# Layer-0 FFN norm by token halves with its differences between the scalings, and a state-space output block moved to a scratch slot

## The reference, cut to what matters

```python
# first block: state-space mixer, then its output projection under a gate
y_ssm = _mamba2_mixer(hn @ w_z, hn @ w_xbc, hn @ w_dt, ...) @ w_ssm_out      # 2048 -> 1024
merged = jax.nn.sigmoid(hn @ w_gs) * y_ssm + jax.nn.sigmoid(hn @ w_ga) * y_nsa

# second block, layer i
x = x + g1 * ox                      # ox: grouped-query attention times gqa_w_out in layer 0
x = x + g2 * conv_ffn(norm_modulate(x, norm2_g[i], sh2, sc2), ffn_w_up[i], ...)
def norm_modulate(h, g, shift, scale): return rms_norm(h, g) * (1 + scale) + shift
def conv_ffn(h, w_up, conv_w, conv_b, w_down):
    u = dwconv_centred(h @ w_up, conv_w, conv_b)          # three taps along the tokens
    val, gate = jnp.split(u, 2, axis=-1)
    return (jax.nn.silu(gate) * val) @ w_down
```

## Time and profile before

| | |
|---|---|
| median of 3 runs | 2077.77 us (2075.35 to 2079.31) |
| profiled execution | 2078.08 us, span 2076.2 us |
| mean granted TensorE clock | 0.979 |
| TensorE busy | 1947.4 us, 94% of the span |
| VectorE, ScalarE, GpSimd busy | 1027.1, 561.2, 59.5 us |
| read from HBM | 354.97 MB, 171 GB/s over the span |
| chain that ended last | PE 88%, DVE 4%, DMA 3%, issue 2% |

### The profile page before, as it was taken

How to read it: one execution, slowest core, us unless ns; L and a number is a source line. 1 busy time by engine, 2 the same in 40 slices (tenths; PEclk the granted TensorE clock), 3 DMA queues, 4 the chain that set the end, 5 groups by cost and what they waited for, 6 DMA issues and landing times.

```text
span 2076.2 us, 27449 instructions
## 1 busy us (share of the span) xinstructions
PE 1947.4 (94%) x9945; PEld 1370.8 (66%) x9945; DVE 1027.1 (49%) x2289; ACT 561.2 (27%) x1177; POOL 59.5 (3%) x68
## 2 busy tenths in 40 slices
PE   5999989779989999999999899999999999999997
PEld 4878777657855555564555388888544465778886
DVE  2466662357532222243477877777697335433311
ACT  3343400144121111131175123333000225344410
POOL 0000000000000000000000000110000010000000
PEclk9999999889999999999999999999999999999999
DMA  9355384141469999940120312223576011134451
GB/s 387 140 188 215 146 346 158 41 183 66 170 257 394 424 425 423 416 187 0 41 82 32 131 61 84 98 81 136 214 261 248 12 63 43 41 142 143 165 194 45
DMA packets 39466, 357.27 MB, mean 172 GB/s; under 512 B 4295, under 2 KB 9038, under 8 KB 10318
## 3 DMA queue, kind: packets, MB, share of 16 engines
q1 hardware_dynamic: 39374, 356.04, 43.7%
HBM read 354.97 MB, written 1.05 MB: 171 GB/s over the span
## 4 chain that ended last, share of the span: by engine, by line
PE 88%; DVE 4%; DMA 3%; issue 2%; ACT 1%; DVEq 1%; PEldq 1%; PEld 1%; SPq 0%; ACTq 0%
PE bank L647 47%; PE bank L1366 13%; PE bank L1144 7%; PE bank L1129 4%; PE bank L1166 4%; PE bank L764 2%; PE bank L1338 1%; PE bank L1248 1%; DMA ring<-in_ada 1%; PE bank L1256 1%; PE bank L1105 1%; PE bank L1345 1%; DMA ring<-in_q 1%; PE bank L867 1%; PEldq L638 1%
## 5 line engine op out<-in xcount | busy, mean ns | idle before, releaser
L647 PE MATMUL bank<-hn,ring 128*128 128x256 f32 (+2 forms) x2080 | 519.5, 410 | 11.6 <-ACT hn L1454 8.0
L647 PE MATMUL bank<-arena,ring 128*128 128x256 f32 (+2 forms) x1600 | 470.1, 451 | 22.1 <-issue 13.8
L647 PEld LDWEIGHTS bank<-hn,ring 128*128 128x128 f32 (+1 forms) x2080 | 398.1, 192 | 121.7 <-issue 66.7
L647 PEld LDWEIGHTS bank<-arena,ring 128*128 128x128 f32 (+1 forms) x1600 | 299.7, 189 | 185.7 <-issue 152.4
L1366 PE MATMUL bank<-hn,ring 128*128 128x256 f32 x704 | 161.0, 382 | 7.4 <-ACT hn L1454 7.4
L1366 PEld LDWEIGHTS bank<-hn,ring 128*128 128x128 f32 x704 | 134.6, 191 | 26.9 <-issue 8.2
L1909 DVE SCALAR_TENSOR_TENSOR bank<-ring,c_rows 128x1024 f32<-128x1024 f32 x96 | 118.1, 1230 | 25.3 <-DMA ring<-in_ada 20.5
L1366 PE MATMUL bank<-ring 128*128 128x256 f32 x528 | 124.1, 386 | 3.2 <-DVEq L2673 3.2
L1909 DVE SCALAR_TENSOR_TENSOR ring<-ring,c_rows 128x1024 f32<-128x1024 f32 x96 | 117.1, 1220 | 0.0
L1366 PEld LDWEIGHTS bank<-ring 128*128 128x128 f32 x528 | 101.7, 194 | 18.9 <-issue 3.9
L1434 ACT ACTIVATE hn<-resid 128x256 f32<-128x256 f32 (+1 forms) x48 | 22.6, 485 | 336.5 <-DVE resid L2000 336.5
(11 more groups left out here) (422 smaller groups left out, 2100.9 us busy)
## 6 DMA issues: line engine op xcount, KB each, us to landing
ring<-in_ada SPq DMA_DIRECT2D x28, 2048.0 KB, 9.4
ring<-in_up SPq DMA_DIRECT2D x44, 1024.0 KB, 4.9
ring<-in_egu SPq DMA_DIRECT2D x20, 2048.0 KB, 10.9
ring<-in_edn SPq DMA_DIRECT2D x39, 1024.0 KB, 9.6
ring<-in_down SPq DMA_DIRECT2D x16, 1408.0 KB, 9.5
arena<-in_egu SPq DMA_DIRECT2D x10, 2048.0 KB, 10.8
hn<-in_egu SPq DMA_DIRECT2D x9, 2048.0 KB, 11.2
ring<-in_adat SPq DMA_DIRECT2D x8, 2048.0 KB, 12.5
```

Of the source, the lines that this page charges most:

```text
L647: last = mm(out, lhs(i), rhs(i), start=i == 0, stop=i == k - 1)
```

## The change

It has four parts.

1. **Slots of the state-space output.** The second pair of `wso`/`gs` lies in slots 4 and 5 instead of 3 and 5, and the `ada2` chunks that VectorE reads beside it go into slot 3 instead of slot 4. `wso` now stands ahead of `gs` in the second round too.
2. **Slots of the attention's output projection.** The `ada2` chunks 7 and 11 go into slot 4 instead of slot 2; since slot 4 is the attention's scratch, SP waits ahead of chunk 7 until all three engines have ended the attention. Slot 2 is then free for the first up weights.
3. **Norm by halves.** The scalings of the layer-0 FFN norm go in the order `up_blocks`: part 0 of k = 0..3, part 1 of k = 0..7, part 0 of k = 4..7. ScalarE shifts each half block and counts it by itself. `up_t1`, now a buffer of its own in the scratch, is computed after 10 of the 16 scalings, `up_t3` after 14, `up_t2` and `up_t4` after all.
4. **First block of seven.** On TensorE the first two blocks are written out ahead of the loop. In the very first, the product of `up_t1` comes second instead of fourth, and VectorE's first `up_second` waits for 4 products instead of 3.

```diff
+        up_t1, up_t2, up_t3, up_t4 = (pl(4, T) for _ in range(4))
+        up_blocks = [(k, 0) for k in range(4)] + [(k, 1) for k in range(KD)] + [(k, 0) for k in range(4, KD)]
...
-            stream(1, [... ("gs", 2, at(0)), ("wso", 0, at(0)), ("adat", 3, at(6)),
-                       ("wso", 3, at(1))])
-            stream(1, [("gs", 5, at(1)), ("ada2", 1, at(0)), ("ada2", 4, at(1)), ("gs", 2, at(2)), ("wso", 0, at(2)),
-                       ("ada2", 1, at(2)), ("gs", 5, at(3)), ("wso", 3, at(3)), ("ada2", 4, at(3))])
+            stream(1, [... ("gs", 2, at(0)), ("wso", 0, at(0)), ("adat", 3, at(6))])
+            stream(1, [("wso", 4, at(1)), ("gs", 5, at(1)), ("ada2", 1, at(0)), ("ada2", 3, at(1)), ("gs", 2, at(2)),
+                       ("wso", 0, at(2)), ("ada2", 1, at(2)), ("wso", 4, at(3)), ("gs", 5, at(3)), ("ada2", 3, at(3))])
...
-                    stream(1, [("gqao", 1, at(0)), ("gqao", 3, at(1)), ("ada2", 0, at(6)), ("ada2", 2, at(7)), ("gqao", 1, at(2)),
-                               ("ada2", 0, at(10)), ("gqao", 3, at(3)), ("ada2", 2, at(11))])
+                    stream(1, [("gqao", 1, at(0)), ("gqao", 3, at(1)), ("ada2", 0, at(6))])
+                    sp.wait_ge(phase, 3 * (GQA_QUERIES + 1))
+                    stream(1, [("ada2", 4, at(7)), ("gqao", 1, at(2)), ("ada2", 0, at(10)), ("gqao", 3, at(3)), ("ada2", 4, at(11))])
...
-            gated_out([(0, 2), (3, 5)], DIN // P, lambda k: ynorm[:, k, :], 0, 2, last_normed)
+            gated_out([(0, 2), (4, 5)], DIN // P, lambda k: ynorm[:, k, :], 0, 2, last_normed)
... TensorE, up projection
+                    if first:
+                        pe.wait_ge(s["up_T"], 1)
+                        product(3, sums[:, 0], lambda k: up_t1[:, k, :])
+                        pe.wait_ge(s["up_T"], 2)
                     product(2, sums[:, 2], lambda k: up_t3[:, k, :])
...
+                if l == 0:
+                    for q in range(2):
+                        up_seven(0, q, q == 0)
+                    with pe.Fori(1, FB // 2) as i:
+                        for q in range(2):
+                            up_seven(i, q, False)
... ScalarE
+                    for x, (k, part) in enumerate(up_blocks):
+                        act_e.wait_ge(s["hn_scaled"], n["hn_scaled"] + x + 1)
+                        half = hn[:, k, part * T:(part + 1) * T]
+                        fn(half, half, ACT.Identity, bias=ada[1][:, 24 + k, part:part + 1]).then_inc(s["hn_ready"], 1)
... VectorE
+                    scaled(0, 10)
+                    ve.wait_ge(s["hn_ready"], nth["up_hn", 0] - 8)
+                    V.tensor_tensor(up_t1, hn[:, 0:4, T:T2], hn[:, 0:4, 0:T], ALU.subtract)
+                    ve.drain().then_inc(s["up_T"], 1)
+                    scaled(10, 14)
+                    ve.wait_ge(s["hn_ready"], nth["up_hn", 0] - 4)
                     V.tensor_tensor(up_t3, hn[:, 4:8, T:T2], hn[:, 0:4, T:T2], ALU.subtract)
                     ve.drain().then_inc(s["up_T"], 1)
+                    scaled(14, 16)
                     V.tensor_tensor(up_t2, up_t3, hn[:, 0:4, 0:T], ALU.add)
                     ve.drain().then_inc(s["up_T"], 1)
+                    ve.wait_ge(s["hn_ready"], nth["up_hn", 0])
                     V.tensor_tensor(up_t4, hn[:, 4:8, 0:T], up_t2, ALU.subtract)
                     ve.drain().then_inc(s["up_T"], 1)
```

More of the change, by code:

```diff
@@ L104 @@
 PI_BELOW = 3.1415925
[L106 removed]
+NSA_QUERIES, MOE_PHASE, GQA_QUERIES, MLA_LOW_RANK, LAST_PHASE = 4, 8, 9, 11, 14
 SETUP_DMAS, REST_DMAS, LATE_DMAS = 1 + VT + 2, 3, 5
@@ L1357, in _, with up_hn, up_seven @@
                 late_norm(w)
-                def up_seven(i, q):
+                if l == 0:
+                    n["hn_ready"] += KD
+                def up_hn(k, part):
+                    pe.wait_ge(s["hn_ready"], n["hn_ready"] - 2 * KD + up_blocks.index((k, part)) + 1)
+                    return hn[:, k, part * T:(part + 1) * T]
+                def up_seven(i, q, first):
                     w, sums = up_weights(q), up_s[q]
@@ L1388, in _ @@
                 nth["up_hn", l] = n["hn_ready"]
-                with pe.Fori(0, FB // 2) as i:
+                if l == 0:
                     for q in range(2):
[L1391 to L1398, removed]
+                        up_seven(0, q, q == 0)
+                    with pe.Fori(1, FB // 2) as i:
+                        for q in range(2):
+                            up_seven(i, q, False)
+                else:
+                    with pe.Fori(0, FB // 2) as i:
+                        for q in range(2):
+                            landed(2 + q, i)
+                            pe.wait_ge(s["ffn_ev"], i * 2 + (n["ffn_ev"] + q + 1))
+                            for x in range(2):
+                                dot(bank[2 * q + x][:, 0:w], lambda k: slot(2 + q)[:, (2 * k + x) * P:(2 * k + x + 1) * P],
+                                    lambda k: hn_block(k)[:, 0:w], KD).then_inc(s["ffn_mm"], 1)
                 free(2, 3)
@@ L2668, in _, with scaled @@
                     up_sums(0, 16 * nth["up", 0, 0])
[L2669 to L2671 removed]
+                    ve.wait_ge(s["std_ready"], norms[0] + 1)
+                    inverse(rstd[:, :], T2, hn[:, KD - 1, :], hn[:, KD - 2, 0:16])
+                    norms[0] += 1
+                    def scaled(first, end):
+                        for k, part in up_blocks[first:end]:
+                            a, b = part * T, (part + 1) * T
+                            V.scalar_tensor_tensor(hn[:, k, a:b], resid[:, k, a:b], mod[1][:, 1, part, k:k + 1], rstd[:, a:b],
+                                                   ALU.mult, ALU.mult).then_inc(s["hn_scaled"], 1)
+                    scaled(0, 10)
[4 more added lines that the diff above has]
+                    ve.wait_ge(s["hn_ready"], nth["up_hn", 0] - 4)
                     V.tensor_tensor(up_t3, hn[:, 4:8, T:T2], hn[:, 0:4, T:T2], ALU.subtract)
                     ve.drain().then_inc(s["up_T"], 1)
+                    scaled(14, 16)
                     V.tensor_tensor(up_t2, up_t3, hn[:, 0:4, 0:T], ALU.add)
                     ve.drain().then_inc(s["up_T"], 1)
[L2676 to L2677 removed]
+                    ve.wait_ge(s["hn_ready"], nth["up_hn", 0])
                     V.tensor_tensor(up_t4, hn[:, 4:8, 0:T], up_t2, ALU.subtract)
                     ve.drain().then_inc(s["up_T"], 1)
[L2680 removed]
+                else:
+                    norm(T, lambda part: mod[2][:, 1, part, :], hn, True)
+                if l == 0:
+                    up_second(0, 0, 4)
                     up_sums(1, 16 * nth["up", 0, 1])
```

39 lines of the change are left out of this document (21 added, 18 removed).

## The result

The changed kernel takes 2067.36 us (median of 7 runs, 2064.2 to 2069.74), the kernel before in the same comparison 2078.01 us (7 runs, 2075.35 to 2083.14): a ratio of 0.9944 with a 95% interval of 0.9931 to 0.9956, so it is faster, by 0.6%. The profiled execution took 2067.65 us, its span 2065.9 us, mean granted clock 0.982 (before: 2078.08, 2076.2, 0.979). In five further runs it took 2063.49 us (2062.31 to 2066.95), ratio 0.993 [0.9916, 0.9943]. The forecast was 2065.0 us. Ratios and intervals are of fast runs alone: of the 19 runs of the kernel before taken beside e1 to e4, one took 2955.76 us at a granted clock of 0.65 and is left out of them.

What follows compares the result with a forecast made beforehand. The prediction took the kernel as bound by TensorE, losing time only where the chain leaves it. State-space output 6.9 plus FFN norm 5.9 gave 12.8 us off 2078.08, forecast 2065.0 us, range 2060.5 to 2070.5.

Steps and rivals of the forecast that it cites:

- State-space output: Second pair of outputs: starts 4.1 us earlier, and no clock fall saves 2.8 us; 6.9 us in all.
- The release: State-space output: TensorE frees slots 4 and 5 for `wso` and `gs` at 255.0, not before VectorE's last scaling at 253.51.
- The landing: State-space output: the 3 MB of `wso` and `gs` take 10.1 us and land at 265.1.
- rival (a): State-space output: late release or landing lets the clock fall; total gain 6 to 9 us, 2069 to 2072 us; chance 0.15.
- FFN norm, the load: Layer-0 FFN norm: first up weights land early, so the inverse starts at 1184.0 instead of 1186.73, 2.75 us.
- (c): FFN norm: weight sums and load were hidden anyway, only the order pays; costs 2.75 us, 2067.8 us; chance 0.05.
- (d): Attention's output projection: SP's new wait delays `ada2` 7, slower if it lands after 1150.1; chance 0.05 with smaller mishaps.
- FFN norm, the order: Layer-0 FFN norm: new sequence ends the first block at 1205.0 instead of 1210.9; 5.9 us together with the load.
- it returns near 1196.9: FFN norm, first block: the clock returns to 2.4 GHz there, after 5.6 to 5.8 us of unbroken work.
- rival (b): FFN norm: the clock holds or returns at once, 7.1 us there; with 7.5 us before it 2063.2 us; chance 0.09.
- from here TensorE has work at any time: FFN norm, first block: TensorE never waits again once `up_t1` runs, from 1191.2 to 1194.7.
- TensorE unbroken from some 6.4 us earlier: FFN norm, sign in the trace: TensorE runs without a break 6.4 us sooner, counted from the last sum of squares.

Runs made afterwards that it cites:

- e1: The kernel before with only the state-space output's slots changed: 2071.82 us (4 runs), ratio to before 0.9957.
- e4: The changed kernel with the state-space output's slots as before, so both norm parts only: 2070.33 us (4 runs), ratio to before 0.995.
- e2: The kernel before with only `ada2` 7 and 11 moved to slot 4, with SP's wait for the attention's end: 2076.16 us (10 runs), ratio 0.9976.
- e7: The changed kernel with the product of `up_t1` fourth again and `up_second` waiting for 3 products: 2067.4 us (4 runs), ratio to before 0.9944.
- e3: The kernel before with only the norm by halves and the new first block, loads untouched: 2078.61 us (10 runs), ratio 0.9993.

## Why the prediction was right

**State-space output, predicted 6.9 us: 7.2 us.** TensorE starts the second pair 14.69 us behind the first, not 19.11: 4.42 us, with 4.1 forecast. The records show 9.91 - 7.14 = 2.77 us of clock, with 2.8 forecast. The stretch to kv is 7.18 us shorter. Inside the first number two errors cancel, and that is luck. The release was taken at 255.0; `wso` left SP at 253.91, right behind VectorE's last scaling (252.05 + 1.67 = 253.72). That is the early bound: TensorE's queue stood at the release while the array was at about record 16 of 64 ((253.91 - 250.45)/0.2195), not at the 24 that stand ahead of it. The landing was taken at 10.1 us from the first issue; it took 265.05 - 253.91 = 11.1 us. The Trainium skill, "DMA: Bandwidth & Descriptors", section "Anatomy of one DMA — SWDGE (gpsimd) path", fits transfers of the GpSimd path and gave an estimate of 9.2 us; this trace does not agree for loads that SP issues, it is 1.9 us longer. Had the release come at 255.0 as assumed, the start would have been 266.2 us, and rival (a) near.

**FFN norm, the load, predicted 2.75 us:** the inverse came 2.8 us earlier against the root (0.02 us behind it in e2 and in the changed kernel, before 2.83), and SP issued `in_up` at 1145.17, by 1152 as said. Rivals (c) and (d) are out: neither was the load hidden, nor did SP's wait reach VectorE.

**FFN norm, the order.** VectorE's sequence was right almost to the tenth. Moved by the 6.59 us that the changed kernel is ahead, `up_t1` starts on TensorE at 1191.2 (forecast 1191.2), `up_t3` at 1194.0 (VectorE done at 1194.0), `up_t2` at 1196.2 (1196.1). The term that was mis-sized is the clock: "it returns near 1196.9". In this frame it was back at 1189.8 in the changed kernel and at 1193.1 in e4. So the product of `up_t2` ended at 1198.2 and not 1199.3, and the block at 1204.05 instead of 1205.0. Both norm parts gave 6.83 us, with 5.9 forecast and 7.1 as the bound for full clock from `up_t1` on. By that the stage went rival (b)'s way, in e4 even with `up_t1` begun at half clock. The reason given for the low clock, that it lasts 5.6 to 5.8 us of unbroken work, came from two stretches; the runs show it back 2.8 us behind the start of the first product in the changed kernel, before that product was over. With it fell the step "from here TensorE has work at any time": behind `up_t1` it waited 0.88 us for `up_t3` and 0.62 us for the third output sum, so of "TensorE unbroken from some 6.4 us earlier" only the start came true (8.02 us behind the last sum of squares, before 14.39). That the end came only 1 us off has a reason: VectorE sets it, and VectorE's times were right.

**Sum.** Forecast 12.8 us. The stages gave 6.59 + 6.78 = 13.4 us (0.6 of the 7.2 was lost again ahead of the norm: 0.2 before the first output, 0.4 behind kv), and the measured medians 10.7 us in the first comparison and 14.7 in the second. The 2065.0 us lies between 2067.36 and 2063.49. That it is only 2.4 us from the first median is in part luck: the stages gave 0.6 us more than forecast, and falls of the clock elsewhere, which no term of the sum holds, took more than that back. The prediction allowed 1.5 us on either side for them; one such fall alone takes 2.9 us.

## What to carry to other kernels

A wait of TensorE can be worth more than its length: starting 4.4 us earlier also saved 2.8 us of half clock behind the wait. When a fill-in order is made (here `up_t1` second), ask which engine ends the stage at either clock: where it is the other engine, the clock costs nothing (e4); where TensorE waits and then has three products in a row, it costs most of what is lost (e7). Judge an edit worth 4 us in 2000 by its stage in the trace, list where the clock was low in the stretches that it can't touch, and don't go by one total: e3 shows the gain in its stage, and its ten runs can't tell it from nothing.

## What the runs showed of the hardware

- The same program, with the same gaps of 1.02 and 0.26 us ahead of the same eight matmuls, lost its clock in one execution (7.06 us) and kept it in another (3.67 us). The Trainium skill, "TensorE: Matmul & The Clock Gate", section "What's actually happening", says that the interval in which activity is judged runs freely and is not started by the kernel. The pair of traces agrees with that; it doesn't prove it.
- At the norm the clock was back 2.8 us behind the start of the first product in the changed kernel and only 6.1 us behind it in e4, with 3.83 us of idle time ahead of that product in both. In e7, with the same 3.83 us ahead but 3.37 us of idle time behind the product, it was 12.9 us.
- TensorE's queue executed a release that stands ahead of record 25 by the time the array was at record 16: SP's load, which waits for it, left 3.46 us behind the first record (3.47 us in e1 and e7), and record 25 starts 5.27 us behind it. So a buffer comes free 1.8 us before the array gets there.
- 2 + 1 MB issued 0.38 us apart landed in 11.1 us here, in 10.75 before, in 11.9 in e2 and in 9.8 beside the output projection.
